# The sum that completes a pair's third quarter, in front of both convolutions instead of between them

## The reference, cut to what matters

```python
h = rms_norm(x, g_pre_ffn)
u = causal_depthwise_conv(h @ w_up.astype(x.dtype), ffn_conv_w) + ffn_conv_b.astype(x.dtype)
gate, val = jnp.split(u, 2, axis=-1)
y = (jax.nn.gelu(gate, approximate=True) * val) @ w_down.astype(x.dtype)
return x + rms_norm(y, g_post_ffn)
```

## Time and profile before

| | us |
|---|---|
| median of 3 runs | 1250.87 |
| lowest, highest | 1247.88, 1253.44 |
| the profiled execution, its own time | 1252.86 |
| its span in the trace | 1251.0 |
| TensorE busy | 1175.9 (94%) |
| VectorE busy | 803.3 (64%) |
| ScalarE busy | 537.2 (43%) |
| GpSimd busy | 389.8 (31%) |

### The profile page before, as it was taken

One profiled execution on the slowest core, in us unless ns is written; L12 is line 12 of the kernel. 1 busy time (PEld: TensorE's weight loads), 2 busy tenths in 40 slices (PEclk: granted clock), 3 DMA queues, 4 the chain that ended last, 5 costly groups with the idle time before them and its releaser, 6 DMA issues.

```text
span 1251.0 us, 16935 instructions
## 1 busy us (share of the span) xinstructions
PE 1175.9 (94%) x5964; PEld 989.0 (79%) x5964; DVE 803.3 (64%) x1123; ACT 537.2 (43%) x972; POOL 389.8 (31%) x352
## 2 busy tenths in 40 slices
PE   6999999998999999994899999999999988999996
PEld 5888888887889888873788888777877776888885
DVE  6332354658777666749677877876687776464547
ACT  5211243556344554335434444534444434453451
POOL 1222000212133333113455667456654731000000
PEclk9999999999899999997899999999999999999999
DMA  7321143455333332220235353544536466986513
GB/s 271 115 96 71 57 125 93 147 143 191 97 114 96 112 89 68 75 94 23 93 144 188 115 202 132 172 159 144 169 134 202 136 235 245 394 313 192 186 49 134
DMA packets 117716, 181.85 MB, mean 145 GB/s; under 512 B 20463, under 2 KB 78607, under 8 KB 113423
## 3 DMA queue, kind: packets, MB, share of 16 engines
q1 hardware_dynamic: 117647, 180.94, 42.9%
HBM read 123.21 MB, written 57.70 MB: 145 GB/s over the span
## 4 chain that ended last, share of the span: by engine, by line
PE 22%; DVE 10%; POOL 10%; DMA 5%; issue 3%; ACT 3%; SPq 1%; POOLq 0%; ACTq 0%; DVEq 0%
DMA conv<-in_w_down 4%; POOL f_conv L2770 3%; POOL conv L2770 3%; DVE f_conv L2580 3%; POOL f_w_raw L2766 3%; PE f_ps_up L2878 3%; PE f_ps_up L2879 3%; PE f_ps_up L2880 3%; DVE f_w L2551 2%; PE sums L2812 2%; PE sums L2814 2%; PE sums L2813 2%; PE sums L2880 2%; PE sums L2879 2%; PE sums L2878 2%
## 5 line engine op out<-in xcount | busy, mean ns | idle before, releaser
L2766 POOL TENSOR_TENSOR f_w_raw<-stage 128x512 f32<-128x512 f32 x44 | 68.5, 1557 | 112.9 <-PE f_ps_up L2814 107.4
L2551 DVE TENSOR_TENSOR f_w<-f_w_raw,f_w 128x512 fp32r<-128x512 f32 (+1 forms) x55 | 65.3, 1206 | 42.8 <-POOL f_w_raw L2766 42.8
L2770 POOL TENSOR_TENSOR conv<-conv 128x512 f32<-128x512 f32 x44 | 63.5, 1443 | 58.3 <-DMA conv<-in_w_down 55.7
L2770 POOL TENSOR_TENSOR f_conv<-f_conv 128x512 f32<-128x512 f32 x44 | 66.0, 1500 | 37.1 <-DMA y_blocks<-f_conv 33.7
L207 PE MATMUL sums<-split,slab_w 128*128 128x512 f32 x192 | 75.9, 395 | 0.5 <-PEq L258 0.5
L209 PE MATMUL sums<-split,slab_w 128*128 128x512 f32 x192 | 74.9, 390 | 0.0
L208 PE MATMUL sums<-split,slab_w 128*128 128x512 f32 x192 | 74.8, 389 | 0.0
L2369 ACT CAST f_w<-f_w_raw 128x512 fp32r<-128x512 f32 (+1 forms) x55 | 43.6, 795 | 67.8 <-POOL f_w_raw L2766 67.7
L2812 PE MATMUL f_ps_up<-split,f_w 128*128 128x512 f32 x176 | 69.1, 393 | 2.1 <-DVEq L2547 1.7
L228 DVE SCALAR_TENSOR_TENSOR conv<-sums,conv_taps,conv 128x1023 f32<-128x1023 f32 (+6 forms) x39 | 46.8, 1199 | 37.4 <-ACT conv L219 36.4
L2580 DVE SCALAR_TENSOR_TENSOR f_conv<-f_ps_up,f_taps,f_conv 128x1023 f32<-128x1023 f32 (+1 forms) x44 | 56.3, 1279 | 20.5 <-ACT f_conv L2437 19.7
(11 more groups left out here) (392 smaller groups left out, 3465.1 us busy)
## 6 DMA issues: line engine op xcount, KB each, us to landing
stage<-in_w_up SPq DMA_DIRECT2D x22, 1024.0 KB, 5.7
y_blocks<-f_conv SPq DMA_DIRECT2D x22, 1024.0 KB, 5.1
conv<-in_w_down SPq DMA_DIRECT2D x11, 1024.0 KB, 7.9
w_down_sums<-conv SPq DMA_DIRECT2D x11, 1024.0 KB, 10.5
stage<-y_blocks SPq DMA_DIRECT2D x40, 256.0 KB, 5.0
f_rest_raw<-y_blocks SPq DMA_DIRECT2D x37, 256.0 KB, 5.3
x_tile<-in_x SPq DMA_DIRECT2D x12, 512.0 KB, 4.2
stage<-in_w_in SPq DMA_DIRECT2D x6, 1024.0 KB, 6.6
```

Source lines behind the costliest of these rows:

```text
L2551: dve.tensor_tensor(out, src, hi.bitcast(F32), ALU.subtract).then_inc(s_lo[name], 1)
L2766: pool.tensor_tensor(raw_sum(m), a, b, op).then_inc(s_add[m], 1)
L2770: pool.tensor_tensor(view(out), view(a), view(b), op).then_inc(signal, 1)
```

## The change

In the loop over the pairs, and once behind it, `c21` is called in front of `convolve(., 0)` instead of between the two convolutions. Nothing is added or removed; no wait changes its condition, and the order on TensorE, ScalarE, GpSimd and the sync queue is the same.

```diff
             for p in range(UP):
                 if p > 0:
+                    c21(p - 1)
                     convolve(p - 1, 0)
-                    c21(p - 1)
                     convolve(p - 1, 1)
                 c11(p)
                 lo_a(p + 1)
...
             for s in range(4):
                 block_low(s)
+            c21(UP - 1)
             convolve(UP - 1, 0)
             block_low(4)
-            c21(UP - 1)
             convolve(UP - 1, 1)
```

## The result

| | before | after |
|---|---|---|
| median of 9 runs each, us | 1245.28 (1241.05 to 1253.44) | 1238.21 (1232.98 to 1241.40) |
| ratio after / before, 95% interval | | 0.9921 (0.9898 to 0.9945) |
| the profiled execution, us | 1252.86 | 1236.57 |

The changed kernel is 0.8% faster: 9.8 us of 1245 by the ratio, 7.1 us by the two medians. The forecast was 9.94 us, and its level of 1240.9 lies 2.7 us above the measured median. The two profiled executions stand 16.29 us apart. That is more than either figure, and the experiments had to say which part of it belongs to the change.

A forecast was written before the change was run, and what follows sets the result against it. Late in the stage a 39.65 us loop through load_down, GpSimd, ScalarE and VectorE was taken to bound TensorE, whose floor is 38.08. Terms -8.66 and -1.28 sum to -9.94: 1250.87 becomes 1240.9 us, range 1237 to 1247.5.

The forecast's parts named there:

- first term: Loop over the pairs: cut from 39.65 to 38.00 us, so TensorE's late double steps lose nothing; -8.66 us.
- The level: Starting point of the sum: median 1250.87 us, with the profiled execution 1.99 us above it.
- GpSimd beside VectorE: GpSimd sums meeting VectorE's work at the shared port: booked at nothing, bounds 2.5 us either way.
- The odd steps: c21 waits 1.18 us for A22, against 1.28 us of old wait that goes; booked at -0.1 us a step.
- The tail: Behind the last pair: 1.28 us of VectorE idle time goes, gated product stored sooner, slot 8 passes it whole; -1.28 us.
- Taken from the first pairs on: Early steps: the shorter loop doesn't use up its slack, so even one 0.3 us longer would be covered.
- nearer -11: Sum if low parts in front of GpSimd's last round shorten it by up to 1.65 us.
- Even steps: VectorE's c21 in front of tile 0 begins when the low parts end, A22 being over already.
- Rival 1: Loop keeps part of its length, 38.4 to 38.8 us; at 38.8, 6.3 us gained, 1244.5; chance 0.15.
- Rival 2: Last load_down(10) doesn't move: total gain 1.6 us, 1249.3; chance 0.11 with other cases of little change.
- Rival 3: A22 holds tile 0, next A11 waits; slower, 1260.1 at 0.5 us beyond in 21 steps; chance 0.06.
- its signs: What would show the slower case: lo_a as the releaser of TensorE at most A11.

The follow-up runs named there:

- before again: The kernel before, unchanged, run and traced once more: 1250.08 us, ratio 1.0013 to its other runs.
- tail only: Kernel before with c21 moved only behind the last pair, the loop's 21 steps as before: 1244.58 us, ratio 0.9986.
- odd only: Kernel before with c21 moved only in the loop's odd steps: 1250.77 us, ratio 1.0020.
- even-only: Kernel before with c21 moved only in the loop's even steps: 1240.43 us, ratio 0.9947.
- the delay in even steps: Changed kernel with three more unused sums, 1.8 us together, in front of c21 in even steps: 1249.89 us, ratio 1.0017.
- loop-only: Kernel before with c21 moved in all 21 loop steps but not behind the last pair: 1235.04 us, ratio 0.9912.
- load first: Kernel before with load_down issued in front of load_up on the sync queue: 1247.72 us, ratio 1.0002.
- load later: Kernel before with load_down issued behind the gated product's store: 1286.0 us, ratio 1.0299.
- whole: Kernel before with the whole change, run again as the measure for its parts: 1236.57 us, ratio 0.9923.
- entry wait: Changed kernel with GpSimd's weight sums of pair 1 waiting for VectorE's low parts: 1233.21 us, ratio 0.9892.
- delay in odd steps: Changed kernel with three more unused sums, 1.8 us together, in front of c21 in odd steps: 1236.49 us, ratio 0.9907.
- The last version: Entry wait kernel with the down-projection's first four block loads issued early, in the last group: 1233.30 us, ratio 0.9875.

## Why the prediction was right, and where it was not

The mechanism of the first term held, and so did its size. What failed is the level that the sum starts from, a term booked at nothing, and what was said of the odd steps and of slot 8.

- The level: the sum starts from 1250.87 us, the median of three runs. Nine runs of the same kernel have 1245.28, 5.6 lower. Set against that, the forecast of 1240.9 is a gain of 4.4 us, where 9.8 were measured by the ratio.
- GpSimd beside VectorE, booked at nothing: it gave 1.16 us.
- The odd steps: 1.18 us of new wait was booked for each. It didn't come.
- The tail: slot 8 was to take the gain whole. It does so only if a contest behind the store ends as before.

**The loop (first term, -8.66).** Measured from pair 1 to pair 20: -9.13, of which 0.47 is one early double step of 38.55 us in before that I had not counted. Against the other traces with the old loop (before again, tail only, odd only) it is -8.2 to -9.1. The even-only kernel has nearly all of it (-8.99), the delay in even steps gives it all back, and the loop's own length is 37.3 to 37.9 us by the estimates above, against the 38.00 of the sum. The bound passed to TensorE, as forecast. "Taken from the first pairs on" held as well.

**The tail (second term, -1.28).** The idle time went, and the last gated product's store was issued 15.58 us behind slot 0 instead of 16.78. But slot 8 isn't tied to it alone, as I wrote. Behind the store come GpSimd's last sums and VectorE's two low parts of blocks 8 and 9, which slow each other. The pair in before, the pair in after, and the four sums with the pair in the loop-only kernel, whose tail is as before (in before the sums took 6.18 us):

```profile
1049.11 4.48 DVE L2608 TENSOR_TENSOR f_rest<-stage,f_rest 128x1024 fp32r<-128x1024 f32 x2 [6.73 <-ACT f_rest L2460]
```

```profile
1032.75 4.46 DVE L2608 TENSOR_TENSOR f_rest<-stage,f_rest 128x1024 fp32r<-128x1024 f32 x2 [6.78 <-ACT f_rest L2460]
```

```profile
1036.82 7.29 POOL L2770 TENSOR_TENSOR f_conv<-f_conv 128x512 f32<-128x512 f32 x4 [34.05 <-DMA y_blocks<-f_conv]
...
1039.50 3.46 DVE L2608 TENSOR_TENSOR f_rest<-stage,f_rest 128x1024 fp32r<-128x1024 f32 x2 [6.68 <-ACT f_rest L2460]
```

Whoever comes first wins 1.0 to 1.1 us from the other, and it goes both ways with either order of the tail. From slot 0 to slot 8 it took, in us:

| | GpSimd first (VectorE's pair 4.3 to 4.6 us) | VectorE first (its pair 3.4 to 3.5 us) |
|---|---|---|
| tail as before | 26.83 to 27.09 (before, before again, load first, load later) | 25.54 to 26.07 (loop only, even only, odd only) |
| tail changed | 25.49 to 25.76 (after, whole, tail only, entry wait, delay in even steps) | 24.66 (delay in odd steps) |

The last version, whose slot 0 doesn't wait, is left out. So with the same outcome of the contest the term is there, some 1.1 to 1.4 us. The contest, which the forecast had not seen, is as large. That the loop without the tail reached slot 8 as soon as the whole change is its luck in this contest. No median shows the term.

**GpSimd beside VectorE (booked at nothing, bounds 2.5).** From pair 20 to slot 0 the kernels with an open loop took 39.7 to 40.5 us, those with a loop of 39.7 us 41.3 to 41.8 (the delay in even steps, which has the new order, is one of these). GpSimd's last round lasted 19.8 us (977.56 to 997.35) instead of 21.0: its weight sums took 0.4 us less, since VectorE's low parts now lie in front of the round, its `y_sums` 0.8 less, and its `down_sums` 7.9 as before. The rule that I had weighed there, from the Trainium skill, SBUF — State Buffer, section "SBUF: two separate sides", gave up to 1.65 us and a sum "nearer -11". The trace agrees in its direction with 1.2 us, and the whole behind pair 1 is -9.13 - 1.16 - 1.18 + 0.10 = -11.4. I should have booked part of it.

**Odd steps (booked at -0.1 a step).** The saving of 1.28 us came and moved nothing, as the odd-only kernel shows. The new wait did not come in the changed kernel. It is right for a loop that stays long, as in this late odd step of the odd-only kernel:

```profile
806.23 0.70 DVE L2599 TENSOR_TENSOR f_ps_up<-f_ps_up,x_tile 128x512 f32<-128x512 f32 x1 [1.14 <-PE f_ps_up L2817]
```

There it is 1.14 to 1.19 us in five odd steps on end, and with the delay in even steps, whose loop is also 39.7 us long, 1.14 to 1.19 in seven. In the changed kernel it went for a reason that I had not seen. The load in the loop reaches GpSimd sooner: its sums of `w_down` begin 5.1 us behind TensorE's A11 of the odd pair (827.65, 832.79) instead of 10.3 (796.43, 806.71). They now lie beside VectorE's low parts of 1.78 and 2.31 us, which took 0.68 and 1.21 before. VectorE reaches `c21` 2.2 us later for that, behind the end of A22. The failed step is that I carried rows of step 11 over to a kernel in which another engine's round had moved. The room for `lo_a` is 1.7 us in the changed kernel. In before it was 2.4 and not 1.9, since `lo_a` took 1.90 us and not 2.4 (two thirds of the pair was too much).

**Even steps.** The forecast had `c21` start when the low parts end. It stands 0.74 us, because VectorE now runs ahead and TensorE's A22 is the later one. That is free: TensorE sets the pace.

**The level.** The forecast hung a difference on 1250.87, the median of three runs. Nine runs of the same kernel give 1245.28, and twenty-nine on another occasion 1247.85. The profiled execution I summed against was one that had entered late, which is why the two traces lie 16.29 us apart and the medians 7 to 10. The claim that the one execution stands 1.99 us above "the median" was no better than those three runs. 9.94 us from the level of nine would have been 1235.3, 2.9 below what came. The range of 1237.0 to 1247.5 holds 1238.21, and the forecast lies only 2.7 us off, by luck: a level 5.6 too high and a gain that came out 2.9 smaller between the medians than forecast stand against each other.

**The rivals.** Rival 1 (the loop keeps part of its length) doesn't hold: no double step is over 38.1. Its 40.34 us had a cause that the trace shows: the load of that group lasted 9.01 us instead of 8.11 (9.04 to 9.46 at the same place in the other traces with a loop of 39.7 us); why that one lasts longer isn't shown. Rival 2 doesn't hold: load_down(10) is issued at 971.79 instead of 990.00, and the round ends at 997.35. Rival 3 had the right mechanism to look at and the wrong margin: the chain has 1.7 us of room, and 1.8 us more on it cost nothing that a run shows. Against its signs, `lo_a` ends no wait of TensorE between pair 2 and pair 20, and `keep_u2` none either. That nothing passes a waiting `c21` (the Trainium skill, TensorE: Matmul & The Clock Gate, section "Architectural detail: the array is 16× 32×32, not 1× 128×128") agrees with the even step: tile 0 begins at 817.58, behind `c21`, though ScalarE's pass for it had ended at 816.56.

## What to carry to other kernels

Find the loop before costing the edit: follow the chain of waits until it returns to the instruction it began with, and compare its length with the bound engine's time for the same work; what an edit inside it is worth is the smaller of the two differences, times the repetitions in which the loop binds. A sum that waits for nothing belongs in front of the work that it would otherwise split, if its result makes a round trip through another engine: 0.62 us of work had cost 1.9. When a loop gets shorter, re-read which transfers and which GpSimd rounds start sooner, since they meet other instructions of VectorE than in the old trace, and take a kernel's level from many runs: a difference between two traces needs milestones ahead of the first changed instruction.

## What was not expected of the hardware

- A sum of GpSimd that began 0.06 us behind a row of VectorE instructions lasted 6.18 us instead of 1.3; begun 0.36 us ahead, it lasted 1.35 and VectorE's row of three took 7.19 us (1.53, 2.28, 3.38) instead of 5.26 (0.68, 2.29, 2.29).
- TensorE's clock after a wait. Behind 3.54 us (before, pair 1) it was granted at 0.50 for 6 us, about 2.8 us of lost work. But behind waits of about the same length at slot 0 it was 0.50 in the kernel with the whole change, run again (3.7 us), and 1.00 in after (3.62 us):

```profile
1007.87:1013.87 6.00, 6.00 (x14) 0.50 1.03 389
```

```profile
1009.28:1015.28 6.00, 6.00 (x26) 1.00 1.05 396
```

  The length of the wait alone doesn't tell which; in the odd-only kernel it was 3.68 us at slot 0, as in the whole, and the clock stayed at 1.00. What it costs depends on the place: at pair 1 it went to the end, at slot 0 the wait for slot 8 took it in, and a little more. The kernel that ran slowly at slot 0 (whole) then stood 0.79 us for slot 8, was granted 1.00 behind it, and took 200.1 us from there to the end. After stood 3.70 us, was granted 0.74 for the next 6 us, and took 201.5.
- The same program has two groups of runs about 6 us apart, 1234.0 to 1235.3 and 1241.2 to 1241.4 in one kernel, which is near the 4.9 us between an early and a late entry.
